# Last expert stage: gather with the picks stationary, both up halves ahead of it, last pass written out

## The reference

```python
def hier_moe(u, w_grp, b_grp, w_exp, b_exp, w1, w3, w2):
    ...
    _, g_sel = lax.top_k(grp_logits, 1)
    ...
    top_val, top_idx = lax.top_k(in_grp, TOP_K_3)
    top_w = jax.nn.softmax(top_val, axis=-1) * p_grp
    ...
    for gi in range(N_GROUPS):
        hid = jax.nn.silu(jnp.einsum('td,edf->tef', t, w1[gi])) * jnp.einsum('td,edf->tef', t, w3[gi])
        hid = hid * gate[:, gi, :, None].astype(hid.dtype)
        out = out + jnp.einsum('tef,efd->td', hid, w2[gi])
    return out.reshape(b, s, d)

# third_block:
    h = h + g2 * hier_moe(u, w_grp[l], b_grp[l], w_exp[l], b_exp[l], w1[l], w3[l], w2[l])
return rmsnorm(h, final_norm)
```

## Time and profile before

| | us |
|---|---|
| median of 3 runs | 2463.42 (2462.71 to 2465.99) |
| the profiled execution, its time | 2463.65 |
| its span in the trace | 2461.6 |
| of the span, from gather(0) to the end | 262.4 (2199.17 to 2461.6) |

### The profile page before, as it was taken

The page is one execution under the profiler, slowest core; times in us unless marked ns, Lnnn a source line. Parts: engine busy times, 40 slices in busy tenths (PEclk is TensorE's granted clock), DMA queues, the critical chain, the costliest instruction groups (busy, mean ns, idle before and its releaser), DMA issues.

```text
span 2461.6 us, 34558 instructions
## 1 busy us (share of the span) xinstructions
PE 2060.4 (84%) x14185; PEld 1144.0 (46%) x14186; DVE 494.8 (20%) x1075; ACT 364.7 (15%) x808; POOL 322.6 (13%) x149
## 2 busy tenths in 40 slices
PE   6986698668768866989869788999989899889788
PEld 5764222112212211322238665889875546455444
DVE  1034411101111100211120474110221301241111
ACT  1231111011111100111111432100011112210001
POOL 4100112222222222221220000000000000002221
PEclk9988799889989988999989978999989999989889
DMA  9665679999999799997974642655534244259994
GB/s 325 169 240 216 278 302 407 426 426 418 408 426 399 313 425 425 380 407 310 414 302 137 222 155 84 225 166 152 183 118 136 103 141 150 104 203 404 410 409 158
DMA packets 183320, 681.49 MB, mean 277 GB/s; under 512 B 15970, under 2 KB 57219, under 8 KB 150224
## 3 DMA queue, kind: packets, MB, share of 16 engines
q1 hardware_dynamic: 179200, 670.02, 69.8%
q0 software_dynamic: 4032, 10.40, 1.7%
q10 hardware_dynamic: 16, 0.02, 0.0%
HBM read 679.33 MB, written 1.06 MB: 276 GB/s over the span
## 4 chain that ended last, share of the span: by engine, by line
PE 65%; DMA 23%; DVE 6%; ACT 3%; SPq 2%; issue 1%; POOL 0%; DVEq 0%; ACTq 0%; POOLq 0%
PE ps L775 33%; DMA scr<-in_w_mlp 13%; PE ps L1153 8%; PE ps L1179 5%; DMA MOD<-in_w_mlp 3%; DMA spare<-in_b_mlp 3%; PE ps L1470 2%; PE ps L1190 2%; DMA HTY<-in_w 2%; PE ps L810 2%; PE ps L854 1%; PE ps L1121 1%; PE ps L1157 1%; PE ps L917 1%; PE ps L1507 1%
## 5 line engine op out<-in xcount | busy, mean ns | idle before, releaser
L1153 PE MATMUL ps<-ring,scr 128*32 128x512 f32 x2208 | 300.2, 693 | 132.2 <-POOL ring L721 131.8
L775 PE MATMUL ps<-ring,HTY 128*128 128x512 f32 (+5 forms) x960 | 326.3, 501 | 3.7 <-ACT HTY L1554 3.7
L721 POOL COPY ring<-scr 128x4096 f32<-128x4096 f32 x62 | 224.1, 3619 | 776.5 <-DMA scr<-in_w_mlp 569.5
L775 PEld LDWEIGHTS ps<-ring,HTY 128*128 128x128 f32 x960 | 174.7, 190 | 152.0 <-issue 136.0
L775 PE MATMUL ps<-HTY,ring 128*128 128x256 f32 (+1 forms) x1072 | 238.3, 385 | 2.0 <-ACT HTY L1554 1.0
L1153 PEld LDWEIGHTS ps<-ring,scr 128*32 128x32 f32 x2208 | 74.1, 122 | 352.5 <-POOL ring L721 180.4
L775 PEld LDWEIGHTS ps<-HTY,ring 128*128 128x128 f32 (+1 forms) x1072 | 205.5, 192 | 33.3 <-ACT HTY L1554 2.7
L2359 DVE TENSOR_SCALAR spare<-ps 128x256 f32<-128x256 f32 x46 | 19.5, 425 | 675.2 <-PE ps L1157 675.2
L1554 ACT ACTIVATE scr<-ps 128x512 f32<-128x512 f32 (+7 forms) x117 | 58.4, 500 | 503.8 <-PE ps L775 401.6
L775 PE MATMUL ps<-ring,scr 128*128 128x128 f32 (+1 forms) x1040 | 121.6, 280 | 1.4 <-DVE scr L2465 1.4
L775 PEld LDWEIGHTS ps<-ring,scr 128*128 128x128 f32 x1040 | 117.5, 192 | 5.2 <-issue 3.3
(11 more groups left out here) (461 smaller groups left out, 1940.4 us busy)
## 6 DMA issues: line engine op xcount, KB each, us to landing
scr<-in_w_mlp SPq DMA_DIRECT2D x94, 2048.0 KB, 25.5
ring<-in_w_mlp SPq DMA_DIRECT2D x34, 2048.0 KB, 20.9
MOD<-in_w_mlp SPq DMA_DIRECT2D x32, 2048.0 KB, 24.3
HTY<-in_w_mlp SPq DMA_DIRECT2D x32, 2048.0 KB, 22.2
ring<-in_w_ada SPq DMA_DIRECT2D x23, 2048.0 KB, 9.1
ring<-in_w_in SPq DMA_DIRECT2D x20, 2048.0 KB, 7.9
ring<-in_w_ff SPq DMA_DIRECT2D x16, 2048.0 KB, 9.5
ring<-in_w SPq DMA_DIRECT2D x16, 2048.0 KB, 16.3
```

The source lines that it names most:

```text
L721: pool.tensor_copy(m1_slabs[j], m1_arrivals[j]).then_inc(moved[j], 1)
L775: mm = pe.matmul(o, lhs(k), rhs(k), start=begin and k == 0, stop=end and k == nk - 1)
L1153: mm = pe.matmul(ps[C1 * c:C1 * (c + 1), 0, :], XG[:, 2 * j + i, :], m1_slabs[j][:, i, BANK * c:BANK * (c + 1)], start=j + i == 0, stop=False)
```

## The change

**The gather** is turned round. PICK3 is now the stationary operand and 512 columns of H move: 4 matmuls of 128 by 512 in place of 16 of 128 by 128. The result has places as rows, so it has to be transposed: ACT copies it to a new buffer XS3 (`slots`), PE makes 8 transposes of every fourth column of it (`turn_tokens`) into the same banks 2 and 3, and ACT copies these to XG3 as before (`gathered`).

**The order of a pass** on PE is now up half 0, up half 1, gather(n + 1), scatter(n - 1), turn_hidden(n), back(n), turn_tokens(n + 1), down(n). On ACT `slots(n + 1)` stands behind the gate, and `gathered(n + 1)` goes behind the way back.

**The last pass** is written out behind the loop. It has no gather, no slots, no turn_tokens, no gathered and no picks; its `down` waits for `down_read` in place of `gather_read`. The loop runs over passes 1 to 7. For that DVE computes one more number, the index of the last pass (LAST3), with one more instruction; the places in `work` and WORK3 move on by one.

What is left out of the diff: the two new semaphores, the moved addresses, the shifted columns of WORK3 with the subtraction, and the same `last_pass` loop bound on DVE.

```diff
@@ -45,7 +45,7 @@
 END1 = OF_PASS + PASSES + 2
 OF_CHOICE = END1
 COUNT3 = OF_CHOICE + PASSES + 2
-THROUGH3 = COUNT3 + 1
+LAST3, THROUGH3 = COUNT3 + 1, COUNT3 + 2
 QUAD_OF = THROUGH3 + QUADS
 WORK_COLUMNS = QUAD_OF + PASSES3 + 2
 
...
@@ -374,6 +374,7 @@
         XG3, YS3 = shaped(flat_bias[:, 0:D], (KT, SLOTS3)), flat_bias[:, D:2 * D]
         m3_slabs = [scr[:, 0:SLAB], scr[:, SLAB:2 * SLAB], scr[:, 9216:9216 + SLAB]] + [ring[:, i, :] for i in range(SLOTS)]
         m3_slabs = [shaped(v, (2, 2, 4, F3)) for v in m3_slabs[0:4]] + [shaped(v, (JOBS, D)) for v in m3_slabs[4:]]
+        XS3 = scr[:, 2 * SLAB:2 * SLAB + D]
         m3_arrivals = [shaped(v, (2, 2, 4, F3)) for v in (MOD[:, 1:5, :].rearrange("p m d -> p (m d)"), HTY)]
 
 
...
@@ -1451,10 +1452,17 @@
                 if not (isinstance(n, int) and n <= 1):
                     pe.wait_ge(m3["down_read"], n - 1)
                 for half in range(2):
+                    for a in range(NT):
+                        mm = pe.matmul(ps[:, 2 + half, :], PICK3[:, a, :], H[:, a, BANK * half:BANK * (half + 1)], start=a == 0, stop=a == NT - 1)
+                    mm.then_inc(m3["gather"], 1)
+
+            def turn_tokens(n):
+
+                for half in range(2):
+                    pe.wait_ge(m3["slots_read"], 2 * n + half + 1)
                     for k in range(4):
-                        mm = mm_k(ps[:, 2 + half, P * k:P * (k + 1)], lambda a: H[:, a, BANK * half + k:BANK * (half + 1):4],
-                                  lambda a: PICK3[:, a, :], NT)
-                    mm.then_inc(m3["gather"], 1)
+                        mm = pe.transpose(ps[:, 2 + half, P * k:P * (k + 1)], XS3[:, BANK * half + k:BANK * (half + 1):4], ident[:, :])
+                    mm.then_inc(m3["turn_tokens"], 1)
 
             def up(n, q, h):
 
...
@@ -1497,9 +1505,12 @@
                     mm = pe.transpose(ps[:, 1, S + P * a:S + P * (a + 1)], PICKG3[:, a, :], ident[:, :])
                 mm.then_inc(m3["back"], 1)
 
-            def down(n, q):
-
-                pe.wait_ge(m3["gather_read"], 2 * n + 4)
+            def down(n, q, last=False):
+
+                if last:
+                    pe.wait_ge(m3["down_read"], n)
+                else:
+                    pe.wait_ge(m3["gather_read"], 2 * n + 4)
                 for c in range(2):
                     pe.wait_ge(m3_landed[4 + c], 16 * q + 16)
                     for half in range(2):
...
@@ -1508,27 +1519,29 @@
                                            m3_slabs[4 + c][:, t, BANK * half:BANK * (half + 1)], start=c == 0, stop=c == 1)
                 mm.then_inc(m3["down"], 1)
 
-            def quad_pass(n, q, first=False):
+            def quad_pass(n, q, first=False, last=False):
 
                 up(n, q, 0)
-                if first:
-                    up(n, q, 1)
+                up(n, q, 1)
+                if not last:
                     gather(n + 1)
-                else:
-                    gather(n + 1)
-                    up(n, q, 1)
+                if not first:
                     scatter(n - 1)
                 turn_hidden(n)
                 back(n)
-                down(n, q)
+                if not last:
+                    turn_tokens(n + 1)
+                down(n, q, last)
 
             gather(0)
+            turn_tokens(0)
             quad_pass(0, 0, first=True)
             pe.wait_ge(m3["listed"], 1)
-            n_passes = pe.value_load(work[0:1, COUNT3:COUNT3 + 1], min_val=QUADS, max_val=PASSES3)
-            with pe.Fori(1, n_passes) as n:
+            last_pass = pe.value_load(work[0:1, LAST3:LAST3 + 1], min_val=QUADS - 1, max_val=PASSES3 - 1)
+            with pe.Fori(1, last_pass) as n:
                 quad_pass(n, pe.value_load(work[0:1, bass.ds(n + QUAD_OF, 1)], min_val=0, max_val=QUADS - 1))
-            scatter(n_passes - 1, last=True)
+            quad_pass(last_pass, QUADS - 1, last=True)
+            scatter(last_pass, last=True)
 
 
         @block.scalar
...
@@ -1911,11 +1924,16 @@
             act.activation(LE[:, :, :], LE[:, :, :], ACT.Exp).then_inc(route_exp, 1)
             read(MASKED3[:, :], product()[:, 0:3 * E3])
 
+            def slots(n):
+                for half in range(2):
+                    act.wait_ge(m3["gather"], 2 * n + half + 1)
+                    act.activation(XS3[:, BANK * half:BANK * (half + 1)], ps[:, 2 + half, :], ACT.Copy).then_inc(m3["slots_read"], 1)
+
             def gathered(n):
                 if not (isinstance(n, int) and n == 0):
                     act.wait_ge(m3_half_used[1], n)
                 for half in range(2):
-                    act.wait_ge(m3["gather"], 2 * n + half + 1)
+                    act.wait_ge(m3["turn_tokens"], 2 * n + half + 1)
                     act.activation(XG3[:, 4 * half:4 * half + 4, :], ps[:, 2 + half, :].rearrange("p (k c) -> p k c", k=4),
                                    ACT.Copy).then_inc(m3["gather_read"], 1)
 
...
@@ -1931,18 +1949,23 @@
                 act.wait_ge(m3["back"], n + 1)
                 act.activation(PT3, ps[:, 1, S:2 * S], ACT.Copy).then_inc(m3["back_read"], 1)
 
-            def quad_pass(n):
+            def quad_pass(n, last=False):
                 gate(n)
+                if not last:
+                    slots(n + 1)
                 turned_hidden(n)
-                gathered(n + 1)
                 way_back(n)
-
+                if not last:
+                    gathered(n + 1)
+
+            slots(0)
             gathered(0)
             quad_pass(0)
             act.wait_ge(m3["listed"], 1)
-            n_passes = act.value_load(work[0:1, COUNT3:COUNT3 + 1], min_val=QUADS, max_val=PASSES3)
-            with act.Fori(1, n_passes) as n:
+            last_pass = act.value_load(work[0:1, LAST3:LAST3 + 1], min_val=QUADS - 1, max_val=PASSES3 - 1)
+            with act.Fori(1, last_pass) as n:
                 quad_pass(n)
+            quad_pass(last_pass, last=True)
             for a in range(NT):
                 act.wait_ge(m3["sum"], a + 1)
                 step(act.activation(Y[:, a, :].rearrange("p (c n) -> p c n", c=2), ps[:, 4 + 2 * a:6 + 2 * a, :], ACT.Square,
...
@@ -2631,18 +2655,20 @@
 
                 dve.wait_ge(m3["sil"], n + 1)
                 tell(dve.tensor_tensor(aS3, ps[:, 0, F3:2 * F3], sil3, ALU.mult), m3["hidden"], n + 1)
-                dve.wait_ge(m3["back"], n + 1)
-                pick_back(n + 1)
-                pick(JOBS * quad_of(n + 2), OFFSET3[:, n + 2:n + 3] if isinstance(n, int) else OFFSET3[:, bass.ds(n + 2, 1)],
-                     n + 2, astep)
+                if not last:
+                    dve.wait_ge(m3["back"], n + 1)
+                    pick_back(n + 1)
+                    pick(JOBS * quad_of(n + 2), OFFSET3[:, n + 2:n + 3] if isinstance(n, int) else OFFSET3[:, bass.ds(n + 2, 1)],
+                         n + 2, astep)
                 dve.wait_ge(m3["down"], n + 1)
                 tell(dve.tensor_tensor(YS3, ps[:, 2:4, :].rearrange("p b n -> p (b n)"), MOD[:, 5, :], ALU.mult), m3["down_read"], n + 1)
-                assert own[0] == QUAD_STEPS, own[0]
+                assert last or own[0] == QUAD_STEPS, own[0]
 
             quad_pass(0)
-            n_passes = dve.value_load(work[0:1, COUNT3:COUNT3 + 1], min_val=QUADS, max_val=PASSES3)
-            with dve.Fori(1, n_passes) as n:
+            last_pass = dve.value_load(work[0:1, LAST3:LAST3 + 1], min_val=QUADS - 1, max_val=PASSES3 - 1)
+            with dve.Fori(1, last_pass) as n:
                 quad_pass(n)
+            quad_pass(last_pass, last=True)
             g = vector()
             for a in range(NT):
                 dve.wait_ge(out_root, a + 1)
```

More of the change, by code:

```diff
@@ L262, in build @@
         m3 = {n: sem("m3_" + n) for n in (
-            "counted", "listed", "masked", "pick", "pick_back", "gather", "gather_read", "sil", "hidden", "turn",
+            "counted", "listed", "masked", "pick", "pick_back", "gather", "slots_read", "turn_tokens", "gather_read", "sil", "hidden", "turn",
             "turn_read", "down", "down_read", "back", "back_read", "sum", "step")}
@@ L368, in build @@
         OFFSET3, WORK3 = borrow3(1142, PASSES3 + 2), borrow3(1168, WORK_COLUMNS - COUNT3)
-        rcur3, gcur3 = borrow3(1203, NT, JOBS), borrow3(1211, NT, JOBS)
+        rcur3, gcur3 = borrow3(1204, NT, JOBS), borrow3(1212, NT, JOBS)
         PICK3, PICKG3 = borrow3(1280, NT, SLOTS3), borrow3(1536, NT, SLOTS3)
@@ L2580, in _ @@
                                    rcur3.rearrange("p a t -> p (a t)").unsqueeze(2).to_broadcast(shape), ALU.is_equal), m3["pick"], 1)
-            through3 = WORK3[:, 1:1 + QUADS]
+            through3 = WORK3[:, 2:2 + QUADS]
             step(dve.tensor_reduce(QCOUNT, count.rearrange("p (q t) -> p q t", t=JOBS), AX.X, ALU.max))
@@ L2590, in _ @@
             step(dve.tensor_copy(WORK3[:, 0:1], through3[:, QUADS - 1:]))
-            tell(dve.tensor_copy(work[:, COUNT3:QUAD_OF], WORK3[:, 0:1 + QUADS]), m3["counted"], 1)
```

(8 more changed lines are left out.)

## The result

| | before | after |
|---|---|---|
| median, us | 2463.07 (2460.91 to 2465.99, 4 runs) | 2446.51 (2444.89 to 2450.43, 4 runs) |
| profiled execution, us | 2463.65 | 2444.89 |
| its span | 2461.6 | 2443.1 |
| first gather begins at | 2199.17 | 2195.34 |
| from there to the end of the span: the stage | 262.4 | 247.8 |

The ratio of the runs is 0.9929, 95% interval 0.9913 to 0.9945.

The account below looks back on a forecast made before the run. PE's work was taken to count only at the start and in passes 6 to 8, hidden by the weight stream between. 2463.65 - 2.2 (pass 6, start's 0.6 included) - 2.1 (pass 7) - 8.3 (pass 8) + 0.2 = 2451.2 us, range 2448 to 2456.

Parts of the forecast that it names:

- What bounds the kernel: Whole kernel: PE's work counts before the weight stream starts and after the last quad but one arrives; in between it is hidden.
- The new gather: Gather on PE: 4 matmuls, 8 records, 3.63 us in place of 7.67, a gain of 4.04 where the clock is high.
- The start: First gather to up: up starts at 2207.0 in place of 2207.59, -0.6 us; bounds 1.6 better, 1.7 worse by the clock.
- The transposes: Eight new transposes of every fourth column: 0.24 us each, 1.9 in all, between bounds of 1.04 and 2.6.
- the gap: From turn_hidden to down: 3.65 us in place of 1.76, +1.9 a pass; in the last pass 1.1, so -0.65.
- Rival (a): Transposes cost as packed ones (0.75 less per gap, 0.9 at the start), or the clock rises at once: 2449; chance 0.08.
- Slab 3: Pass 6: up half 1 waits for this weight slab until 2381.5, not 2381.0; the pass still ends 2.2 us earlier.
- slab 5: Pass 8: down needs this last weight slab at 2434.7, slack 0.8 us, by the slowest row 1.4 late; 0.2 taken.
- (b): Pass 8: slab 5 is late by its upper row, or the way out of the loop costs time; 2452.5 to 2454, chance 0.12.
- (c): The clock falls in the gap from turn_hidden to down, 4.2 us over passes 6 and 7; 2455.4, chance 0.05.
- (d): Clock stays at 1.2 GHz through the passes because each now has two waits; about 2520, slower, chance 0.03.
- (e): The gather isn't faster with H moving, 7.67 us stays and the transposes come on top; 2462.3, chance 0.04.

Follow-up runs that it names:

- Gather twice: The changed kernel with every gather's four matmuls made twice; stage 256.7 us against 246.1 for the changed kernel at the same clock.
- after again: The changed kernel run once more with no edit; 2447.65 us, ratio 0.9935 to the kernel before, stage 246.1 us.
- packed slots: The changed kernel with ACT writing XS3 in packed order, so the eight transposes read packed columns; stage 246.5 us, pass 7 20.52.
- the gather alone: The kernel before with only the new gather and its transposes, old up order, last pass still in the loop; stage 253.7 us, ratio 0.996.
- the last pass alone: The kernel before with only the last pass written out without its gather, old gather and order kept; stage 254.5 us, ratio 0.9975.
- packed gather: The kernel before with the old gather's stationary columns packed instead of every fourth, token features in the wrong order; stage 247.9 us.

## Why the prediction was right, and where it was wrong

**What bounds the kernel** was right: start and passes 6 to 8 count, the rest is under the stream. Gather twice shows it term by term. The trace of after has the passes 3 to 5 at 30.7 us, as before, though each has 3 us less work on PE.

**The new gather**, 3.63 us: right to the last digit. **The start**: forecast 7.83 from the first gather to up, measured 7.45; the clock did as it had in the trace of before. In after again it did not, and the start was 5.82, 0.4 below the forecast's own bound for the high clock (7.83 - 1.6 = 6.23). This clock is a matter of the execution, which one trace could not tell.

**The transposes** are the step that failed. Between the bounds of 1.04 and 2.6 us for eight I took 1.9, from the spacing of the old gather at the same step; they took 1.12. The row was the nearest in its step, but not in its kind: a record of a float32 matmul loads its stationary operand at 329 ns and spaces at 0.24 with it, a transpose at 210 and spaces at 0.14. The row of the transposes at step 2, 196 ns, was the nearer one, and packed slots confirms that the step is worth 0.05 us for eight. So the gap was 3.00, not 3.65, and this term alone makes 0.65 too much in each of passes 6 and 7 and most of the 0.4 at the start: 1.6 us in all. Rival (a), at 0.08, was the case in its first half, and by its price, 2.4 us on top of the 12.4, the stage would have given 14.8 against 14.7 measured. That it comes so close is in part luck: the transposes were worth 1.6, and the smaller terms made up the rest.

**Smaller terms.** The scatter takes 3.43 us behind the gather where it took 3.63 behind up, and two up halves in a row 6.87, not 7.00: some 0.2 us seem to go with each change between stationary operands of 32 columns and of 128, and the new order has fewer of them (no run took this apart). That is 0.3 in pass 7. Slab 3 holds pass 6 as forecast (6.45 us behind its start, 6.2 forecast), and slab 5 came in time, where 0.2 had been put. In all the stage gave 14.7 where 12.4 were forecast.

**The other 2.4 us** between 2451.2 and 2446.51 are not in the stage as the first pair of traces has it. 0.6 of them are the base, 2463.65 where the median is now 2463.07. Where the other 1.8 lie is open: ahead of the stage, or in the start of the runs without a trace, if their first gather found the high clock (the stage then gives 16.3, by after again). I had made the range of the costs in the stage alone and taken 2463.65 as given, from three runs that lay within 3.3 us. 29 runs of the same kernel lay within 12, and 2.4 us of such a difference could be put down to the granted clock in code that the change doesn't touch. By the stage's 14.7 alone the time is 2463.07 - 14.7 = 2448.4, inside the range.

**The range** does not follow from its own terms. Those that it names give 2451.2 - 1.6 = 2449.6 to 2451.2 + 1.7 + 1.4 + 1.2 = 2455.5, and for the transposes it names only the dear bound. With the packed one at rival (a)'s price (0.75 in each of two gaps, 0.9 at the start) the low end is 2447.2. That still misses 2446.51: a range of two medians has to hold their spread too.

**The parts** don't add up: 8.7 for the gather and 7.9 for the last pass make 16.6, and both together give 14.7, since the gather's 2.8 in pass 8 are won only once. That leaves 13.8, and of the 0.9 beyond it 0.3 stand in pass 7 (20.57 against 20.90 with the gather alone). 0.5 of it is what the last pass alone had been short of, since with the new order slabs 2 and 3 of the last quad come sooner. With the old gather the order was worth nothing over the whole stage.

**The rivals.** (b) did not come: no matmul in pass 8 waits for a DMA, and down follows turn_hidden by 1.2 us (2425.89 to 2427.09), 1.1 forecast. It was close: the last part of slabs 4 and 5 landed 12.5 us behind its issue, at 2428.4, and down reads it from about 2428.8. (c) did not come: the clock in the gap is 1.00 with ten transposes in 2.2 us. The Trainium skill, page TensorE: Matmul & The Clock Gate, Part 4, has it that transposes don't count as busy in the way that matmuls do; in this trace the clock doesn't fall over them. (d) did not come: the wait for slab 3 is 0.30 us, and the clock is 1.00 through passes 7 and 8. (e) did not come: the gather takes 3.63.

The rule of 16-byte cachelines (the Trainium skill, page Advanced Engine Details and Errata, section Memory Cachelines) agrees with the packed gather, 192 ns a load in place of 329. But it doesn't give the price. The same step makes a transpose's load longer too, 210 ns in place of 141, and costs the transposes' spacing next to nothing; the sum that I had tied to it was the worse one.

## What to carry to other kernels

When a stationary operand is read at a step, try the packed order before turning the product round: one subscript halved this gather where the clock is high. But something has to write the operand in that order, and here that cost DVE 1.6 us or ACT's copy 0.5. What is saved on the engine under a full weight stream is worth nothing here (3 us of it in each of passes 3 to 5 left them at 30.7); look for what runs before the stream starts and behind the last arrival, and for work that the last iteration of a loop does for a next one that doesn't come. To price a new instruction take the row of its own kind, even at another step, before one of another kind at the same step; and put the spread of whole executions into the range, not only the costs of the stage. Before comparing a short stage in two traces, look at the granted clock at its start in both.

## What the runs showed that I had not expected

- A float32 matmul record with 128 stationary columns at a step of 16 bytes is spaced 0.24 us at either clock level; packed, 0.12 at 2.4 GHz and about 0.22 at 1.2 GHz (13 records in the first 2.77 us of packed gather, the granted clock 0.50). So packing pays mostly at the high level. A transpose at the same step is spaced 0.14, packed 0.13.
- The granted clock behind a like wait was 0.50 in one execution and 1.00 in the next, for the same code: the first gather took 5.34 or 3.70 us.
- Up half 0 behind the long wait took 6.15 us in the changed kernel and 5.66 before: the low level lasted longer. The length of the wait doesn't explain it: 6.92 us and 4.80 there, but a wait of 9.25 in packed gather left it at 5.10. In the changed kernel it is hidden, since slab 3 lands later. Up half 0 of pass 6 in packed gather (timeline of PE):

```profile
2370.92 5.10 PE L1470 MATMUL ps<-scr,BIAS 128*32 128x512 f32 x32 [9.25 <-POOL scr L752]
```

- Strided operands on the other engines: DVE's tensor_tensor of 128 by 1024 took 1.99 us in place of 1.22, ACT's copy of 128 by 512 1.08 in place of 0.60.
